# Thirty convolution taps go from ten early pieces to the ten pieces of the attention heads

## The reference, cut to what matters

```python
xn = rms_norm_2(h, g_mix); proj = xn @ w_in
u_conv, q, k, v, gate_conv, gate_attn = split(proj)
a, gate = split(u_conv);  z = a * sigmoid(gate)
y = causal depthwise convolution of z, 31 taps, 512 channels
conv_o = silu(layer_norm(y + b_dw)) @ w_conv_out
attn_o = sliding_window_attention(q, k, v, sinks) @ w_attn_out     # 8 heads
h = h + (sigmoid(gate_conv) * conv_o + sigmoid(gate_attn) * attn_o) @ w_out
h = h + hierarchical_moe(rms_norm_2(h, g_ffn), ...)
```

## Time and profile before

| what | value |
| --- | --- |
| median of 3 runs | 2753.43 us (2752.44 to 2759.17) |
| profiled execution, whole | 2757.18 us |
| its span, first to last instruction | 2755.2 us |
| TensorE, busy | 2007.1 us (73%) |
| VectorE, busy | 1475.7 us (54%) |
| GpSimd, busy | 1197.3 us (43%) |
| DMA, mean over the span | 352 GB/s, 970.70 MB |
| chain that ended last | DMA 32%, PE 31%, DVE 14%, POOL 10% |

### The profile page before, as it was taken

How to read it: one execution, slowest core, us unless ns; L and a number is a source line. 1 busy time by engine, 2 the same in 40 slices (tenths; PEclk the granted TensorE clock), 3 DMA queues, 4 the chain that set the end, 5 groups by cost and what they waited for, 6 DMA issues and landing times.

```text
span 2755.2 us, 36985 instructions
## 1 busy us (share of the span) xinstructions
PE 2007.1 (73%) x14519; PEld 1251.1 (45%) x14519; DVE 1475.7 (54%) x3358; ACT 487.1 (18%) x816; POOL 1197.3 (43%) x1389
## 2 busy tenths in 40 slices
PE   5999576688496875688946388748599878867753
PEld 3666463445054451355523166333287544434331
DVE  2777899743784286763562686792136232222213
ACT  2203211021111410104310101210113111111101
POOL 1111356666665766665665655675500012212212
PEclk8999898899697987799977589879799989989976
DMA  8996689999999999999999989999854568999996
GB/s 314 338 364 223 257 330 403 405 391 368 409 386 403 409 401 406 385 403 383 388 395 351 358 304 362 365 395 383 338 188 136 191 265 353 409 428 400 403 428 274
DMA packets 244823, 970.70 MB, mean 352 GB/s; under 512 B 28029, under 2 KB 30181, under 8 KB 232391
## 3 DMA queue, kind: packets, MB, share of 16 engines
q0 software_dynamic: 193696, 696.80, 65.9%
q1 hardware_dynamic: 44688, 265.32, 24.1%
q10 hardware_dynamic: 6296, 6.57, 0.7%
HBM read 951.92 MB, written 16.68 MB: 352 GB/s over the span
## 4 chain that ended last, share of the span: by engine, by line
DMA 32%; PE 31%; DVE 14%; POOL 10%; issue 7%; ACT 3%; SPq 1%; POOLq 0%; DVEq 0%; ACTq 0%
PE psum L203 19%; DMA arena<-in_peer_v_dram,arena 11%; POOL arena L456 10%; DMA y_slots<-arena 8%; DVE arena L468 5%; PE psum L563 5%; DMA arena<-in_w_up_dram 5%; DMA arena<-in_peer_u_dram,arena 4%; DMA arena<-in_ada_w_dram 1%; PE psum L2505 1%; DMA arena<-in_hgrn_w_in_dram 1%; DVE arena L668 1%; DMA arena<-in_w_in_dram 1%; PE psum L1456 1%; PE psum L2516 1%
## 5 line engine op out<-in xcount | busy, mean ns | idle before, releaser
L203 PE MATMUL psum<-arena 128*128 128x256 f32 (+2 forms) x3776 | 973.4, 419 | 124.3 <-DMA arena<-in_hgrn_w_in_dram 31.7
L203 PEld LDWEIGHTS psum<-arena 128*128 128x128 f32 x3776 | 708.8, 198 | 392.8 <-issue 222.4
L468 DVE CUSTOM_DVE_ANT_0 arena<-arena,psum 128x1024 f32<-128x1024 f32 x512 | 596.2, 1216 | 115.1 <-DMA arena<-in_peer_u_dram,arena 113.7
L456 POOL DMA_INDIRECT arena<-in_peer_v_dram,arena x512 | 498.1, 973 | 307.5 <-PE psum L563 151.8
L456 POOL DMA_INDIRECT arena<-in_peer_u_dram,arena x512 | 493.9, 965 | 284.2 <-issue 139.0
L563 PE MATMUL psum<-arena 128*32 128x512 f32 x2048 | 317.6, 751 | 239.5 <-DMA arena<-in_peer_v_dram,arena 236.3
L2580 POOL DMA_DIRECT2D y_slots<-arena x188 | 93.4, 497 | 401.0 <-DVE arena L2566 377.1
L563 PEld LDWEIGHTS psum<-arena 128*32 128x32 f32 x2048 | 68.9, 125 | 432.4 <-issue 426.0
L2505 PE MATMUL psum<-arena 128*32 128x256 f32 x3008 | 192.1, 412 | 72.1 <-DMA arena<-in_w_up_dram 62.2
L2505 PEld LDWEIGHTS psum<-arena 128*32 128x32 f32 x3008 | 102.9, 119 | 147.4 <-issue 96.0
L2566 DVE COPY arena<-psum 128x256 f32<-128x256 f32 x47 | 19.9, 424 | 257.7 <-DMA y_slots<-arena 251.7
(11 more groups left out here) (386 smaller groups left out, 2020.7 us busy)
## 6 DMA issues: line engine op xcount, KB each, us to landing
arena<-in_w_gate_dram SPq DMA_DIRECT2D x32, 2048.0 KB, 19.3
arena<-in_w_up_dram SPq DMA_DIRECT2D x32, 2048.0 KB, 23.7
arena<-in_w_down_dram SPq DMA_DIRECT2D x32, 2048.0 KB, 16.3
arena<-in_ada_w_dram POOLq DMA_DIRECT2D x20, 2048.0 KB, 11.0
arena<-in_hgrn_w_in_dram SPq DMA_DIRECT2D x10, 2048.0 KB, 14.0
arena<-in_kv_w_dram POOLq DMA_DIRECT2D x8, 2048.0 KB, 13.8
arena<-in_w_in_dram POOLq DMA_DIRECT2D x7, 2048.0 KB, 12.5
arena<-in_w_in_dram SPq DMA_DIRECT2D x7, 2048.0 KB, 8.0
```

Of the source, the lines that this page charges most:

```text
L203: last = pe.matmul(o, lhsT=lhs(k), rhs=rhs(k), start=start and k == 0, stop=stop and k == n - 1)
L456: pool.indirect_dma_start(RING(n, k), None, (U_TAB, V_TAB)[v], bass.IndirectOffsetOnAxis(ap=at, axis=0))\
L468: last = dve.tensor_tensor_reduce(out=row, in0=row, in1=bank(XB0, 0, D), scale=1.0, scalar=0.0, op0=ALU.mult, op1=ALU.add, accum_out=par_s ...
```

## The change

The first half's table of taps. Ten early pieces (8 to 17) had three taps each, the ten pieces of the heads (18 to 27) nine, piece 28 four. Now the early pieces have none, the heads' pieces twelve, piece 28 four as before. Nothing else differs.

```diff
-        TAP_SEGS = ({8 + i: 3 for i in range(10)} | {18 + i: 9 for i in range(10)} | {28: 4}, {7: 9, 8: 9, 9: 9, 18: 9, 19: 8} | {10 + i: 10 for i in range(8)})
+        TAP_SEGS = ({18 + i: 12 for i in range(10)} | {28: 4}, {7: 9, 8: 9, 9: 9, 18: 9, 19: 8} | {10 + i: 10 for i in range(8)})
```

## The result

Over 20 runs of each, the changed kernel takes 2759.82 us (median) and the kernel before 2751.36: +8.5 us, a ratio of 1.003 with a 95% interval of 1.002 to 1.0039. The forecast of 2759.5 is met, but the kernel before was 2 us faster in these runs than in the three that the forecast started from, so that the loss is 8.5 us where 6.05 were forecast, and it lies on the bound of 0.3% itself. The profiled execution took 2762.89 us, its span is 2760.8; between the two profiled executions the difference is 5.7 us.

The account below looks back on a forecast made before the run. DMA bounds the quarter, except 1758 to 1800 us, where the heads' own chain does. 0 - 0 + 2.48 + 3.57 = +6.05 us on the median of 2753.43 gives 2759.5 us; range 2748 to 2766.

Parts of the forecast that it names:

- Taken from the early pieces: Early pieces, 1643 to 1698 us: removing 11.9 us of VectorE's taps is worth 0.
- Heads 0 to 3: First four attention heads: 4.75 us of added taps, all hidden; the wait before 1754.98 shrinks from 6.88 to 3.31 us.
- Heads 4 to 6: Next three heads: 3.57 us of added taps, less the idle of 1.09 us before 1775.87, leaves +2.48 us.
- Heads 7 to 9: Last three heads: 3.57 us of added taps count in full; the second tile's first dot product starts at 1795.4.
- What GpSimd does of it: GpSimd in the heads: held gathers end with the longer burst; it leaves the last at about 1796.3, some 6.1 us late.
- first rival: Heads: longer bursts do not hold GpSimd longer; only the release at 1773.37 is late: +2.4 us, 2755.8; chance 0.22.
- Behind 1800: After 1800 us, with DMA at share 1.03 up to 1896: no delay is given back, +6.05 us at the end.
- third rival: Heads: no cover holds, DMA has gaps before 1758 too, all ten heads count: +11.9 us, 2765.3; chance 0.20.

## Why the prediction was right, and where it was not

Taken from the early pieces, 0: right. The run with the thirty taps behind the last dots gives 0.9998, and in the kernel after the idle time before the first scores grew from 16.67 to 19.74 us, the waits among the early dots from 1.23 and 1.96 to 4.52 and 4.78.

Heads 0 to 3, hidden: right in the result, and more than forecast by luck. The wait before head 4, forecast to shrink to 3.31 us, went altogether, and head 4 started at 1751.65 and not at 1754.98, 3.33 us earlier. The rows landed 0.67 us earlier (the sum starts at 1748.63 and not at 1749.30); the sum then took 1.92 us where it took 3.64, and the scores 1.13 where they took 2.07. TensorE's granted clock was 0.50 from 1749.3 to 1754.9 in the kernel before, after a wait of 3.17 us, and 1.00 from 1748.6 to 1751.6 in the kernel after, after one of 0.88. The prediction has no term for the clock.

Heads 4 to 6, +2.48 us: this is the term that failed in its reason and in its size. Head 7 started 4.54 us later. The idle of 1.09 us before it, which was to take its part, grew to 5.41 us instead: the sum ahead of it waited 5.50 us for rows that GpSimd had issued late, after three gathers of 3.25 us. The prediction sees VectorE's work ahead of the transposes here and gives the holding no part.

Heads 7 to 9, +3.57 us: right in this profile, 8.09 - 4.54 = 3.55.

What GpSimd does of it: the mechanism was right, the size too small, and it was given the wrong place. The held gathers end 0.88 to 0.90 us behind the run of instructions that holds them, as read; the last one ends at 1798.3 (1796.3 forecast). But the step counted only that GpSimd comes out of the last burst as late as VectorE. In fact every burst from head 3 on holds a gather, and the gathers lose 10.3 us more in all than in the profile before. How much of the 8.5 us this is, the experiments bound and do not fix: 7.9 us between the added three instructions and the added reduction; about 2.7 if the 5.8 us that the change cost with broken bursts on both sides were all VectorE's. For a longer chain without longer holding the prediction's first rival gave +2.4 us, and the reduction measured +2.1. So part of the agreement of the forecast with the time is chance: the wait before head 4 fell away, the one before head 7 grew.

Which bursts hold a gather, and for how long, is told by the runs: with the second operand in PSUM no burst of taps does (the longest gather of the heads is 1.37 us), and a reduction with one SBUF input ahead of nine taps lengthens no holding (2.07 us with it and without). The holding lasts to the end of the run of instructions and not for one tap of 0.396 us: the gather of 6.03 us waited from 1792.28 to 1797.42 for taps alone, about 13 of them, and the one at 1772.20 (2.68 us) on through the product behind its burst. The first rival's premise, that longer bursts do not hold GpSimd longer, is refuted: the last burst went from 18 to 24 taps, and the gather that it holds from 3.65 to 6.03 us.

Behind 1800, nothing given back: nearly right, 8.1 us late at the first dots and 1977.76 against 1971.28, 6.5 us, at the last gather of the quarter, so that 1.6 us were given back. The third rival was right in one point: DMA does fall short ahead of 1758 as well, 373 GB/s instead of 401.

## What to carry to other kernels

Before instructions with two SBUF operands are gathered into a run on VectorE beside GpSimd's indirect DMAs, look at the longest of those DMAs in the profile and at where it ends; if it ends a fixed time behind the run (here 0.88 to 0.90 us), the length of the run has a price of its own beside VectorE's time. Here a one-column memset after every third of them, or an operand in PSUM, took the holding away: the longest gather of the heads fell from 6.03 us to 1.19 and to 1.37. To see what is left without it, take it away on both sides of the comparison. And when an experiment changes results on which later work depends, count that work before its time is believed.

## What was not expected of the hardware

A memset of one column between taps adds about 0.01 us to VectorE (1.20 us for three taps and the memset, 1.19 for three taps) and lets the waiting gather through (none of the heads is over 1.19 us); why it is enough, and why the first one to three gathers that start in a burst pass with 0.93 to 1.25 us and only the next is held, no run here tells. A tap takes the same time with its second operand in PSUM (9.47 us for 24) as in SBUF (9.57).
